# The attention output product of the second layer as one level of Strassen

## The chip, the cores and the metric

The kernel runs on one core of one Trainium2 chip. It is one launch that computes two layers. The metric is device time in microseconds, the median of the runs of one kernel.

## The reference

512 tokens of width 1024, all float32. The first layer is a differential attention beside a bidirectional retention, an output product and a residual. The second layer is the one that the change touches, cut to what matters here:

```python
h = rms_norm(x, norm_g)
u = h @ w_in
v_c, b_c, c_c, z_c, q, k, v, z_a, gate_logits = split(u)
y_c = b_c * causal_depthwise_conv(c_c * v_c, conv_w) * silu(z_c)
y_a = y_c @ w_conv_out
o = sliding_window_attention(rms(q), rms(k), v, sinks) * silu(z_a)   # 512 x 1024
y_b = o @ w_attn_out                                                 # 1024 x 1024 weights
gates = sigmoid(gate_logits + gate_b)
g_a, g_b = split(gates)
return x + (g_a * y_a + g_b * y_b) @ w_out
```

## The kernel before, in words

**Products.** Every large product is taken from float32r parts: a number is split into hi (rounded) and lo (the rest), and `products` issues three matmuls, hi x hi, hi x lo and lo x hi. TensorE works through the weights in pieces of 512 KB, numbered `n`; a piece is 24 matmuls. Four pieces make a unit `u`. Units 0 to 13 are the projections of both layers and the output product of the first. Units 14 to 21 (`U_CONV`, pieces 56 to 87) are the convolution branch, 22 and 23 (`U_AOUT`, pieces 88 to 95) the attention output product, 24 and 25 (`U_COUT`, 96 to 103) the convolution output product. In these pieces one matmul has 512 columns, the tokens, and a piece gives 128 of the 1024 output columns. From piece 104 (`GATES`) on, the gate product and the last output product are already done as one level of Strassen, with 7 products of half size where 8 blocks would be needed: a gate piece has matmuls of 256 columns (tokens), again 24. Sums of weight blocks for these lie in a DRAM scratch, `w_sums`, four blocks of 512 x 512 for each group (groups 0 and 1 the gates, 2 the last product).

**The way of a weight piece.** SP loads it into one of 4 ring slots (more from the gate stage on) as soon as `piece_done` says that the piece 4 before it is done, GpSimd rounds it to hi (`round_piece`, L723), VectorE subtracts for lo (`split_piece`, L1142), and TensorE waits for `w_split`. From piece 110 on ScalarE rounds (`round_block`, L835). Rounding and split of piece n+3 stand in the program at piece n.

**The order of the other work.** It is written by hand: every piece has two halves, and `STEPS` lists for each half the steps (transposes, scores, attention products) that TensorE does after it and that the other engines serve in the same order. The second layer's sliding window attention has 16 steps k = 0 to 15, one for each three halves from piece 53 (`WIN_FIRST`) on. In phase 0 TensorE does the scores S2 of step k and then AV2, the product with the values, of step k-2; in phase 1 TP, the transposes of the probabilities of step k-1. After TP, ScalarE and VectorE take the transposes as hi and lo, and GpSimd masks them (`part_keys`, L734 and L738: one select each for hi and lo where there is one key tile, two each otherwise); AV2 waits for that by `pT_split`. The steps OS at pieces 80 to 83 split the gated attended values `gT2` into `o2_hi` and `o2_lo`.

**The sums of weight blocks.** SP copies blocks of w_in_2 and w_out_2 into `w_sums` (`copy_block`, L666, 1 MB each) at pieces 20 to 27 and 48 to 51 (`COPY_AT`). GpSimd then adds blocks to them by DMAs that accumulate (`gather`, L751, 1 MB each), four steps for each group, one at the end of every third piece from 56 to 89 (`SUM_AT`). From step 2 of a group on, `gather` waits until the earlier steps of the group have landed:

```python
if step >= 2:
    pool.wait_ge(w_gathered[group], 16 * step)
source = (w_block(group, 0, 1), w_sums[4 * group], w_block(group, 0, 1), w_sums[4 * group + 1])[t]
pool.dma_start(w_sums[4 * group + t], source, accum_op=ALU.add).then_inc(w_gathered[group], 16)
```

**Banks.** Tiles of a plain unit go to the four banks of `proj`; ScalarE evacuates those of U_AOUT to `y_b` and of U_COUT to `part` with a factor of 0.5 (L968). The gate products use all eight banks in turn (`gate_banks`).

Of the kernel before, what the change touches and what calls it, by code (L numbers as in the profile page):

```python
# [30 lines left out]
P = 128  # L31
# [26 lines left out]
U_AOUT = U_CONV + KC  # L58
U_COUT = U_AOUT + KC // 4
UNITS = U_COUT + KC // 4  # L60
GATES = 4 * UNITS
# [7 lines left out]
GROUPS = 3  # L69
# [27 lines left out]
def slot_of(n):  # L97

    if n < GATES:
        return n % SLOTS  # L100
    return RING + n - GATES if n < GATES + EARLY else (n - GATES - EARLY) % RING
# [15 lines left out]
def unit_columns(u):  # L117
# [10 lines left out]
    if u < U_AOUT:  # L128
        t = u - U_CONV
        return TRA, [("w_in_2", c + P * t) for c in (CV, CC, CB, CZ)]  # L130
    t = 4 * ((u - U_AOUT) % (KC // 4))
    return TRA, [("w_attn_out_2" if u < U_COUT else "w_conv_out_2", P * (t + j)) for j in range(4)]

# [12 lines left out]
X_AGAIN_AT = range(4 * U_O0 + 3, 4 * U_O0 + 7)  # L146
XS_HOOKS = (7, 7, 8, 9)
# [117 lines left out]
def tiles_done(n, half):  # L265

    u, q = divmod(n, 4)
    if n >= GATES:
        return []
# [5 lines left out]
def build(nc, a):  # L275
    with ExitStack() as ctx:
# [121 lines left out]
        m_hi = sb("m_hi", [P, KC, S], F32R, stack=later)  # L398
        logit = sb("logit", [P, 2, 2, 2, 256], stack=later)
# [35 lines left out]
        v_sum = spare[:, 0:2, 256:512]  # L435

# [10 lines left out]

        def pair_of(t, c, r):

            return t[:].rearrange("p (h k) s -> p k h s", h=2)[:, c, :, r * 256:r * 256 + 256]  # L450

        def w_block(group, row, col):

            w, c = (("w_in_2", G2), ("w_in_2", G2 + D), ("w_out_2", 0))[group]
# [14 lines left out]
        def ring_parts(n, i):  # L469

            t = ring(n)[i]
            if n >= FINAL:
# [3 lines left out]
        def sources(n):  # L476

            if n >= FINAL:
# [5 lines left out]
        def wait_room(eng, n):  # L484
# [7 lines left out]
            elif n >= GATES:  # L492
                eng.wait_ge(piece_done, 4 * U_COUT)
# [41 lines left out]
        hi_done = sem("hi_done"); block_hi_done = sem("block_hi_done")  # L535
# [42 lines left out]
        w_copied = sem("w_copied"); w_gathered = [sem(f"w_gathered{i}") for i in range(GROUPS)]  # L578
        minus_done = sem("minus_done"); low_landed = [sem(f"low_landed{i}") for i in range(len(LOW_BY_DMA))]
        sx_summed = sem("sx_summed"); sx_hi_done = sem("sx_hi_done"); sx_split = sem("sx_split")  # L580
# [8 lines left out]
        def wait_tile(eng, u, j):  # L589
# [3 lines left out]
            else:  # L593
                eng.wait_ge(piece_done, 4 * u + j + 1)
# [20 lines left out]

        N_PARAMS = 18
# [4 lines left out]
        def _(sp):  # L621
            def load_piece(n):
                u, q = divmod(n, 4)
                raw, landed = ring(n)[0], raw_landed[slot_of(n)]
                if n >= GATES:
# [37 lines left out]
            def copy_block(i):  # L663

                t, group = divmod(i, GROUPS)
# [1418 lines left out]
```

## Time and profile before

| what | us |
|---|---|
| median of 3 runs (816.49 to 817.74) | 817.2 |
| the profiled execution, its own time | 816.7 |
| its span, first to last instruction | 814.7 |
| TensorE busy | 808.5 |
| VectorE busy | 609.4 |
| ScalarE busy | 321.9 |
| GpSimd busy | 182.6 |

The profile is of one execution. Its times count from the start of the span. Matmuls are pipelined and their ends are modelled, so the duration of one matmul in the profile is longer than the distance from one to the next; the distance is what a matmul costs. Instructions that issue a DMA count as no busy time.

### The profile page before, as it was taken

The numbers are of one execution on the slowest core, as the hardware profiler recorded it, in microseconds if no ns is written. First come the engines' busy times: TensorE is split into PE (matmuls) and PEld (weight loads), VectorE is DVE, ScalarE is ACT, GpSimd is POOL, SyncE is SP. The second block draws the span as 40 slices with busy tenths as digits, with TensorE's granted clock in tenths as the row PEclk, the third lists the DMA queues.
The fourth block names the chain that finished last, engine by engine and source line by source line (L and its number), as shares of the span: only waits on it lengthen the run. The fifth ranks groups of instructions, "written<-read, shape, count | busy, mean of one in ns | idle before, by whom it ended". The sixth has DMA issues, their size and how long they took to land.

```text
span 814.7 us, 11429 instructions
## 1 busy us (share of the span) xinstructions
PE 808.5 (99%) x4220; PEld 687.1 (84%) x4220; DVE 609.4 (75%) x1096; ACT 321.9 (40%) x701; POOL 182.6 (22%) x189
## 2 busy tenths in 40 slices
PE   9999999999999999999999999999999999999998
PEld 7778888888888888888888888888888888999986
DVE  4998778768984476885579788978952269599998
ACT  4374465632212255334445554441000122355580
POOL 2212111111111221121324445444323224000000
PEclk9999999999999999999999999999999999999999
DMA  7332214445143222653365555566876335866562
GB/s 239 87 97 77 79 52 153 158 157 179 53 155 126 82 83 77 208 175 90 91 130 130 125 119 120 128 130 155 168 165 158 104 88 145 233 182 183 182 205 78
DMA packets 129565, 108.92 MB, mean 134 GB/s; under 512 B 4525, under 2 KB 101350, under 8 KB 129510
## 3 DMA queue, kind: packets, MB, share of 16 engines
q1 hardware_dynamic: 123142, 95.60, 38.4%
q0 software_dynamic: 6336, 12.58, 9.4%
q8 instruction: 34, 0.56, 0.3%
q14 instruction: 21, 0.17, 0.1%
q10 hardware_dynamic: 32, 0.01, 0.0%
HBM read 106.08 MB, written 27.26 MB: 164 GB/s over the span
## 4 chain that ended last, share of the span: by engine, by line
PE 92%; DVE 5%; issue 1%; ACT 1%; DVEq 0%; ACTq 0%
PE proj L1736 24%; PE proj L1738 24%; PE proj L1737 24%; PE bank_t L1750 3%; PE bank_o L1825 2%; DVE x L1447 1%; DVE w_lo L1142 1%; PE score L1738 1%; PE score L1737 1%; PE score L1736 1%; PE score L1900 1%; PE score L1899 1%; PE score L1811 1%; PE score L1810 1%; PE bank_o L1918 1%
## 5 line engine op out<-in xcount | busy, mean ns | idle before, releaser
L723 POOL TENSOR_SCALAR w_hi<-w_raw 128x1024 fp32r<-128x1024 f32 x109 | 128.8, 1182 | 436.2 <-DMA w_raw<-in_w_in_dram 310.8
L1142 DVE TENSOR_TENSOR w_lo<-w_raw,w_hi 128x1024 fp32r<-128x1024 f32 x145 | 179.9, 1244 | 60.2 <-POOL w_hi L723 59.6
L1736 PE MATMUL proj<-xt_hi,w_hi 128*128 128x512 f32 (+1 forms) x448 | 171.1, 382 | 0.0
L1738 PE MATMUL proj<-xt_hi,w_lo 128*128 128x512 f32 (+1 forms) x448 | 168.1, 375 | 0.0
L1737 PE MATMUL proj<-xt_lo,w_hi 128*128 128x512 f32 (+1 forms) x448 | 167.8, 375 | 0.0
L1738 PEld LDWEIGHTS proj<-xt_hi,w_lo 128*128 128x128 f32 x448 | 84.4, 188 | 15.5
L1737 PEld LDWEIGHTS proj<-xt_lo,w_hi 128*128 128x128 f32 x448 | 84.5, 189 | 14.2
L1736 PEld LDWEIGHTS proj<-xt_hi,w_hi 128*128 128x128 f32 x448 | 84.5, 189 | 13.9
L1736 PE MATMUL proj<-w_hi,xt_hi 128*128 128x512 f32 x152 | 61.0, 401 | 0.2 <-ACT prob L922 0.2
L1738 PE MATMUL proj<-w_hi,xt_lo 128*128 128x512 f32 x152 | 59.5, 392 | 0.0
L1737 PE MATMUL proj<-w_lo,xt_hi 128*128 128x512 f32 x152 | 59.4, 391 | 0.0
L835 ACT ACTIVATE w_hi<-w_raw 128x1024 fp32r<-128x1024 f32 x36 | 36.9, 1049 | 9.6 <-DMA w_raw<-w_sums 3.8
L1736 PE MATMUL proj<-w_hi,yc_hi 128*128 128x512 f32 x96 | 38.9, 406 | 0.0
L1738 PE MATMUL proj<-w_hi,yc_lo 128*128 128x512 f32 x96 | 37.6, 392 | 0.0
L1737 PE MATMUL proj<-w_lo,yc_hi 128*128 128x512 f32 x96 | 37.4, 390 | 0.0
L1736 PEld LDWEIGHTS proj<-w_hi,xt_hi 128*128 128x128 f32 x152 | 28.6, 188 | 6.9 <-ACT prob L922 0.7
L1038 ACT ACTIVATE prob<-prob,neg_mx 128x512 f32<-128x512 f32 x32 | 22.9, 716 | 28.3 <-DVE neg_mx L1546 28.3
L1080 ACT ACTIVATE prob<-prob,neg_m 128x128 f32<-128x128 f32 x64 | 25.0, 391 | 22.3 <-DVE sink_m L1652 22.3
L1738 PEld LDWEIGHTS proj<-w_hi,xt_lo 128*128 128x128 f32 x152 | 28.5, 188 | 6.2
L1737 PEld LDWEIGHTS proj<-w_lo,xt_hi 128*128 128x128 f32 x152 | 28.6, 188 | 6.0 <-issue 0.2
L734 POOL TENSOR_SCALAR_AFFINE_SELECT yc_hi<-pT 128x512 fp32r<-128x512 f32 x28 | 17.6, 646 | 71.4 <-ACT pT L1094 71.4
L1543 DVE CUSTOM_DVE_ANT_0 prob<-score,table 128x512 f32<-128x512 f32 x32 | 20.8, 688 | 16.1 <-PE score L1811 16.1
(420 smaller groups left out, 1774.4 us busy)
## 6 DMA issues: line engine op xcount, KB each, us to landing
w_raw<-in_w_in_dram SPq DMA_DIRECT2D x79, 512.0 KB, 3.8
w_sums<-in_w_in_dram SPq DMA_DIRECT2D x8, 1024.0 KB, 7.5
w_raw<-w_sums SPq DMA_DIRECT2D x32, 256.0 KB, 3.3
w_raw<-in_w_out_dram SPq DMA_DIRECT2D x14, 512.0 KB, 3.3
w_raw<-in_w_in_dram SPq DMA_DIRECT2D x26, 256.0 KB, 3.6
w_sums<-w_sums POOLq DMA_DIRECT2D x6, 1024.0 KB, 9.9
w_sums<-in_w_out_dram SPq DMA_DIRECT2D x4, 1024.0 KB, 6.8
w_sums<-in_w_in_dram POOLq DMA_DIRECT2D x4, 1024.0 KB, 9.9
```

Source lines behind the costliest of these rows:

```text
L723: pool.tensor_scalar(hi, raw, 1.0, 1.0, ALU.mult, ALU.mult).then_inc(hi_done, 1)
L734: pool.affine_select(out=pT_hi[:, c, :, :], in_=pT[:, 0, :, :], compare_op=op, fill=0.0, base=base, pattern=pattern, channel_multiplier=step)
L835: act.activation(hi, raw, ACT.Copy).then_inc(block_hi_done, 1)
L1038: act.activation(prob[:, m % 2, mp, :], prob[:, m % 2, mp, :], ACT.Exp, bias=neg_mx[:, m % 2, mp:mp + 1], accum_out=den[:, m % 2, mp:mp + ...
L1080: act.activation(prob2[:, m % 2, r, 0:P], prob2[:, m % 2, r, 0:P], ACT.Exp, bias=neg_m2[:, m % 4, r:r + 1], accum_out=den2[:, m % 4, r:r + 1])
L1142: dve.tensor_tensor(lo, raw, hi.bitcast(F32), ALU.subtract).then_inc(w_split, 1)
L1543: dve.tensor_tensor_reduce(prob[:, sl, mp, :], score[:, mp, :], table[:, h % 2, CENTRE - i * P:CENTRE - i * P + S], 1.0, -3e38, ALU.subtra ...
L1736: pe.matmul(out, left[0], right[0], start=first, stop=False)
L1737: pe.matmul(out, left[0], right[1], start=False, stop=False)
L1738: return pe.matmul(out, left[1], right[0], start=False, stop=last)
L1750: last = pe.transpose(dst, src, ident[:])
L1825: last = pe.matmul(bank_o[:, i * P:(i + 1) * P], wT[:, m % 2, c * P:(c + 1) * P], va[:, c, h * P:(h + 1) * P], start=(c == 0), stop=(c == 3))
```

## The change

The attention output product becomes one level of Strassen. It has 14 pieces instead of 8, 88 to 101: two pairs, each with the 7 products in the order of `OUT_ORDER`. Each piece gives 2 x 128 output columns for 256 tokens over 512 of the 1024 rows, 24 matmuls of 256 columns (`attended_product`). The convolution output is then pieces 102 to 109, and the gates begin at 110. The unit U_AOUT is gone.

- Weights: a fourth group (`ATTENDED`) of block sums of w_attn_out_2. All 16 copies stand at pieces 12 to 27. All 16 gathers stand at pieces 53, 54, 56, 57, 59, 60 and so on to 75, the new group first. SP waits for that group's gathers before it loads piece 88.
- The 14 pieces are rounded by ScalarE (`round_out`), the rest as before.
- Attended values: ScalarE takes the hi copies of OS from VectorE, for 256 tokens only in chunks 0 to 3. VectorE forms four sums of quarters in place (`attended_sum`, pieces 85 to 87), ScalarE rounds them (pieces 87 and 88), VectorE takes their low parts (`attended_low`, pieces 88 to 90). The factor 0.5 of the evacuation moves into the gating (0.25).
- Results: VectorE adds up the products from PSUM into `y_b` (`combine_out`), ScalarE copies the first of each pair (`take_first_out`).
- Waits for banks and for the end of this stage move accordingly.

```diff
-U_AOUT = U_CONV + KC
-U_COUT = U_AOUT + KC // 4
+U_COUT = U_CONV + KC
 UNITS = U_COUT + KC // 4
-GATES = 4 * UNITS
+AOUT = 4 * U_COUT
+OUT_PIECES = 7 * 2
+COUT = AOUT + OUT_PIECES
+GATES = 4 * UNITS + OUT_PIECES
...
+OUT_ORDER = [A11, A12, A22, S2, S1, S4, S3]
+GROUPS = 4
+ATTENDED = 3
...
-COPY_AT = [*range(4 * U_GA, 4 * U_O0), *range(4 * U_Z0, 4 * U_Z1)]
-SUM_AT = [4 * U_Z1 + 4 + 3 * i for i in range(4 * GROUPS)]
+COPY_AT = range(4 * U_RQK, 4 * U_O0)
+GROUP_ORDER = [ATTENDED, 0, 1, 2]
+SUM_AT = [4 * U_Z1 + 1 + 3 * i // 2 for i in range(4 * GROUPS)]
...
+SO_SUM_AT = ((AOUT - 3, 1), (AOUT - 2, 0), (AOUT - 2, 1), (AOUT - 1, 0))
+SO_HI_AT = ((AOUT - 1, 0), (AOUT - 1, 1), (AOUT, 0), (AOUT, 1))
+SO_LOW_AT = ((AOUT, 0), (AOUT, 1), (AOUT + 1, 1), (AOUT + 2, 1))
...
+        def sum_of_attended(product):
+            place = {S2: 0, S1: 1, S4: 2}
+            if product == S3:
+                return [quarter(t, 1, 0) for t in (o2_hi, o2_lo)]
+            return [t[:, 4 * place[product]:4 * place[product] + 4, :] for t in (so_hi, so_lo)]
+        def left_of_attended(product):
+            source, chunk, token = LEFT[product]
+            if source:
+                return sum_of_attended(product)
+            return [t[:, chunk:chunk + 4, token:token + 256] for t in (o2_hi, o2_lo)]
...
+                pair, i = divmod(n - AOUT, 7)
+                return [right_of(ATTENDED, OUT_ORDER[i])[:, 256 * pair:256 * pair + 256].rearrange("(k p) c -> p k c", p=P)]
...
+        def out_bank(x):
+            return gate_banks[(x + SLOTS) % 8]
...
-                t, group = divmod(i, GROUPS)
-                sp.dma_start(w_sums[4 * group + t], w_block(group, *((0, 0), (1, 1), (1, 1), (1, 0))[t])).then_inc(w_copied, 16)
+                group, t = GROUP_ORDER[i // 4], i % 4
+                sp.dma_start(w_sums[4 * group + t], w_block(group, *((0, 0), (1, 1), (1, 1), (1, 0))[t])).then_inc(w_copied[group], 16)
...
+                if n == AOUT:
+                    sp.wait_ge(w_gathered[ATTENDED], 16 * 4)
...
-                group, step = divmod(i, 4)
+                group, step = GROUP_ORDER[i // 4], i % 4
                 t = (0, 2, 1, 3)[step]
-                if i == 0:
-                    pool.wait_ge(w_copied, 16 * 4 * GROUPS)
+                if step == 0:
+                    pool.wait_ge(w_copied[group], 16 * 4)
                 if step >= 2:
                     pool.wait_ge(w_gathered[group], 16 * step)
...
-                            round_piece(m)
+                            if not AOUT <= m < COUT:
+                                round_piece(m)
...
+            def round_out(n):
+                raw, hi, _ = ring(n)
+                act.wait_ge(raw_landed[slot_of(n)], 16 * landings(n))
+                wait_room(act, n)
+                act.activation(hi, raw, ACT.Copy).then_inc(out_hi_done, 1)
...
+            def take_first_out(pair):
+                act.wait_ge(yc_done, KC)
+                if pair:
+                    act.wait_ge(out_combined, COMBINED[S2])
+                act.wait_ge(piece_done, AOUT + 7 * pair + 1)
+                act.activation(u_sum, out_bank(7 * pair), ACT.Copy).then_inc(out_first, 1)
...
+                    if (n, half) in SO_HI_AT:
+                        product, after_sums = ((S2, 3), (S1, 1), (S4, 4), (S3, 2))[SO_HI_AT.index((n, half))]
+                        act.wait_ge(so_summed, after_sums)
+                        act.activation(sum_of_attended(product)[0], raw_sum(product), ACT.Copy).then_inc(so_hi_done, 1)
+                    if half == 1 and AOUT <= n + SPLIT_AHEAD < COUT:
+                        round_out(n + SPLIT_AHEAD)
+                    if half == 1 and AOUT <= n < COUT:
+                        if (n - AOUT) % 7 == 0:
+                            take_first_out((n - AOUT) // 7)
...
+                        elif kind == "OS":
+                            act.wait_ge(o2_gated, WIN_STEPS)
+                            tokens = slice(0, 256 if m < 4 else S)
+                            act.activation(o2_hi[:, m, tokens], gT2[:, m, tokens], ACT.Copy).then_inc(o2_hi_done, 1)
...
+            def attended_sum(i):
+                x11, x12, x21, x22 = (quarter(gT2, row, col) for row in range(2) for col in range(2))
+                if i == 0:
+                    dve.wait_ge(o2_split, KC)
+                    dve.tensor_tensor(x22, x22, x21, ALU.subtract).then_inc(so_summed, 1)
+                elif i == 1:
+                    dve.wait_ge(so_summed, 1)
+                    dve.tensor_tensor(x21, x11, x21, ALU.subtract).then_inc(so_summed, 1)
+                elif i == 2:
+                    dve.wait_ge(so_summed, 2)
+                    dve.scalar_tensor_tensor(out=x11, in0=x22, scalar=-1.0, in1=x11, op0=ALU.mult, op1=ALU.subtract).then_inc(so_summed, 1)
+                else:
+                    dve.wait_ge(so_summed, 3)
+                    dve.scalar_tensor_tensor(out=x12, in0=x12, scalar=-1.0, in1=x11, op0=ALU.mult, op1=ALU.subtract).then_inc(so_summed, 1)
...
+            def attended_low(i):
+                product = (S2, S1, S4, S3)[i]
+                dve.wait_ge(so_hi_done, i + 1)
+                hi, lo = sum_of_attended(product)
+                dve.tensor_tensor(lo, raw_sum(product), hi.bitcast(F32), ALU.subtract).then_inc(so_split, 1)
...
+            def combine_out(x):
+                pair, i = divmod(x, 7)
+                product = OUT_ORDER[i]
+                if product in (A11, A22):
+                    return
+                psum, kept = out_bank(x), out_bank(7 * pair + OUT_ORDER.index(A22))
+                def out(r, h):
+                    return y_b[:, 4 * h + 2 * pair:4 * h + 2 * pair + 2, 256 * r:256 * r + 256]
+                dve.wait_ge(piece_done, AOUT + x + 1)
+                if product == A12:
+                    dve.wait_ge(out_first, pair + 1)
+                else:
+                    dve.wait_ge(out_combined, 7 * pair + COMBINED[product] - (2 if product == S3 else 1))
+                if product == A12:
+                    dve.tensor_tensor(out(0, 0), u_sum, psum, ALU.add).then_inc(out_combined, 1)
+                elif product == S2:
+                    dve.tensor_tensor(w_sum, u_sum, psum, ALU.add).then_inc(out_combined, 1)
+                elif product == S1:
+                    dve.wait_ge(so_split, 4)
+                    dve.tensor_tensor(v_sum_out, w_sum, psum, ALU.add).then_inc(out_combined, 1)
+                elif product == S4:
+                    dve.scalar_tensor_tensor(out=out(0, 1), in0=v_sum_out, scalar=-1.0, in1=psum, op0=ALU.mult, op1=ALU.subtract).then_inc(out_combined, 1)
+                elif product == S3:
+                    dve.scalar_tensor_tensor(out=out(1, 1), in0=v_sum_out, scalar=-1.0, in1=psum, op0=ALU.mult, op1=ALU.subtract).then_inc(out_combined, 1)
+                    dve.tensor_tensor(w_sum, w_sum, psum, ALU.add).then_inc(out_combined, 1)
+                    dve.wait_ge(out_combined, 7 * pair + 6)
+                    dve.tensor_tensor(out(1, 0), w_sum, kept, ALU.add).then_inc(out_combined, 1)
...
-                        done(dve.tensor_copy(o2_hi[:, m, :], gT2[:, m, :]))
-                        dve.tensor_tensor(o2_lo[:, m, :], gT2[:, m, :], o2_hi[:, m, :].bitcast(F32), ALU.subtract).then_inc(o2_split, 1)
+                        dve.wait_ge(o2_hi_done, m + 1)
+                        tokens = slice(0, 256 if m < 4 else S)
+                        dve.tensor_tensor(o2_lo[:, m, tokens], gT2[:, m, tokens], o2_hi[:, m, tokens].bitcast(F32), ALU.subtract).then_inc(o2_split, 1)
...
+            def attended_product(x):
+                n = AOUT + x
+                product = OUT_ORDER[x % 7]
+                wait_low(n)
+                if x == 0:
+                    pe.wait_ge(o2_split, KC)
+                if x < 4:
+                    wait_evacuated(pe, U_COUT - 1, x)
+                elif x < 6:
+                    pe.wait_ge(score2_read, WIN_STEPS)
+                elif x == 6:
+                    pe.wait_ge(pT_split, WIN_STEPS)
+                elif x == 7:
+                    pe.wait_ge(o2_summed, 2 * WIN_STEPS)
+                else:
+                    wait_combined_out(x - 8)
+                if x < 7 and LEFT[product][0]:
+                    pe.wait_ge(so_split, (S2, S1, S4, S3).index(product) + 1)
+                left = left_of_attended(product)
+                w = [ring_parts(n, i)[0] for i in (1, 2)]
+                for j in range(2):
+                    for k in range(4):
+                        last = products(out_bank(x)[:, j, :], [t[:, k, j * P:(j + 1) * P] for t in w], [t[:, k, :] for t in left], k == 0, k == 3)
+                last.then_inc(piece_done, 1)
...
-                if x < 2:
-                    pe.wait_ge(score2_read, WIN_STEPS)
-                elif x == 2:
-                    pe.wait_ge(pT_split, WIN_STEPS)
-                elif x == 3:
-                    pe.wait_ge(o2_summed, 2 * WIN_STEPS)
-                elif x < 8:
+                if x == 0:
+                    pe.wait_ge(out_combined, OUT_PIECES)
+                if 4 <= x < 8:
```

## Rows read from the trace of the kernel before

**Rows 1.** The page's busy times: engine, us, share of the span, instructions

```profile
PE 808.5 (99%) x4220; PEld 687.1 (84%) x4220; DVE 609.4 (75%) x1096; ACT 321.9 (40%) x701; POOL 182.6 (22%) x189
```

**Rows 2.** The table by stage: busy us and instructions per engine, clock, DMA

```profile
403.80:548.90 145.10, 145.10 (x716) 121.89 (x715) 119.54 (x222) 72.89 (x241) 66.10 (x78) 1.00 0.58 127
548.90:604.60 55.70, 55.70 (x249) 46.15 (x248) 43.26 (x54) 3.75 (x7) 20.86 (x18) 1.00 0.71 156
```

**Rows 3.** TensorE in order of time (start us, us), two stage starts

```profile
604.61 0.39 PE L1736 MATMUL proj<-o_hi,w_hi 128*128 128x512 f32 x1
...
648.13 0.39 PE L1736 MATMUL proj<-yc_hi,w_hi 128*128 128x512 f32 x1
```

**Rows 4.** TensorE in order of time, gate products 0 and 9

```profile
691.65 0.28 PE L1736 MATMUL score<-xt_hi,w_hi 128*128 128x256 f32 x1
...
717.56 0.28 PE L1736 MATMUL score<-sx_hi,w_hi 128*128 128x256 f32 x1
```

**Rows 5.** The chain that ended last, share of the span by engine

```profile
PE 92%; DVE 5%; issue 1%; ACT 1%; DVEq 0%; ACTq 0%
```

**Rows 6.** The DMA issues: queue, count, KB each, median us to landing

```profile
w_raw<-w_sums SPq DMA_DIRECT2D x8, 512.0 KB, 3.5
```

**Rows 7.** The page's costliest groups: busy us, mean ns, idle before

```profile
L1142 DVE TENSOR_TENSOR w_lo<-w_raw,w_hi 128x1024 fp32r<-128x1024 f32 x145 | 179.9, 1244 | 60.2 <-POOL w_hi L723 59.6
...
L835 ACT ACTIVATE w_hi<-w_raw 128x1024 fp32r<-128x1024 f32 x36 | 36.9, 1049 | 9.6 <-DMA w_raw<-w_sums 3.8
```

**Rows 8.** Groups of VectorE by line, 652 to 733 us

```profile
L1348 DVE TENSOR_TENSOR sx_lo<-sx,sx_hi 128x1024 fp32r<-128x1024 f32 x4 | 5.6, 1398 | 0.1
...
L1367 DVE TENSOR_TENSOR acc<-th,bank_t 128x512 f32<-128x512 f32 x1 | 0.7, 689 | 1.1 <-PE bank_t L1738 1.1
```

**Rows 9.** SP's copies into w_sums, time from issue to landing

```profile
DMA to landing us min/median/max: 6.1/7.3/8.6
```

**Rows 10.** GpSimd in order of time around piece 63

```profile
449.46 1.06 POOL L751 DMA_DIRECT2D w_sums<-w_sums  x1
450.18 1.43 POOL L723 TENSOR_SCALAR w_hi<-w_raw 128x1024 fp32r<-128x1024 f32 x1
456.68 1.22 POOL L734 TENSOR_SCALAR_AFFINE_SELECT yc_hi<-pT 128x512 fp32r<-128x512 f32 x2 [5.07 <-ACT pT L1094]
457.86 1.22 POOL L738 TENSOR_SCALAR_AFFINE_SELECT yc_lo<-pT 128x512 fp32r<-128x512 f32 x2
```

**Rows 11.** GpSimd's gathers, all twelve, and then those of 445 to 540 us

```profile
L751 POOL DMA_DIRECT2D w_sums<-in_w_in_dram x4: 1056/1067/1209, 406.6 to 513.1; - x4
...
DMA to landing us min/median/max: 9.0/9.9/12.1
...
DMA to landing us min/median/max: 9.4/9.8/10.1
```

**Rows 12.** GpSimd in order of time around pieces 69 and 75

```profile
490.42 2.20 POOL L738 TENSOR_SCALAR_AFFINE_SELECT yc_lo<-pT 128x512 fp32r<-128x512 f32 x2
492.57 1.06 POOL L751 DMA_DIRECT2D w_sums<-in_w_in_dram  x1
...
533.95 1.05 POOL L751 DMA_DIRECT2D w_sums<-w_sums  x1
```

**Rows 13.** TensorE in order of time: second attention products, AV2

```profile
420.68 0.40 PE L1918 MATMUL bank_o<-yc_hi,v 128*128 128x512 f32 x1
...
461.89 0.40 PE L1918 MATMUL bank_o<-yc_hi,v 128*128 128x512 f32 x1
...
504.01 0.40 PE L1918 MATMUL bank_o<-yc_hi,v 128*128 128x512 f32 x1
...
545.18 0.39 PE L1918 MATMUL bank_o<-yc_hi,v 128*128 128x512 f32 x1
```

**Rows 14.** SP's load at 450.6 us, and its load at 437.4 us, to landing

```profile
DMA to landing us min/median/max: 9.7/9.7/9.7
...
DMA to landing us min/median/max: 3.8/3.8/3.8
```

More of the change, by code:

```diff
@@ L127, in unit_columns @@
             (TRA, [("w_in_2", Z2 + 512 + P * j) for j in range(4)])][u]
-    if u < U_AOUT:
+    if u < U_COUT:
         t = u - U_CONV
         return TRA, [("w_in_2", c + P * t) for c in (CV, CC, CB, CZ)]
-    t = 4 * ((u - U_AOUT) % (KC // 4))
-    return TRA, [("w_attn_out_2" if u < U_COUT else "w_conv_out_2", P * (t + j)) for j in range(4)]
+    return TRA, [("w_conv_out_2", P * (4 * (u - U_COUT) + j)) for j in range(4)]
 UNIT = [unit_columns(u) for u in range(UNITS)]
@@ L577, in build @@
         act_chain = sem("act_chain"); dve_chain = sem("dve_chain"); pool_chain = sem("pool_chain")
-        w_copied = sem("w_copied"); w_gathered = [sem(f"w_gathered{i}") for i in range(GROUPS)]
+        w_copied = [sem(f"w_copied{i}") for i in range(GROUPS)]; w_gathered = [sem(f"w_gathered{i}") for i in range(GROUPS)]
         minus_done = sem("minus_done"); low_landed = [sem(f"low_landed{i}") for i in range(len(LOW_BY_DMA))]
+        o2_hi_done = sem("o2_hi_done")
+        so_summed = sem("so_summed"); so_hi_done = sem("so_hi_done"); so_split = sem("so_split")
+        out_first = sem("out_first"); out_combined = sem("out_combined")
         sx_summed = sem("sx_summed"); sx_hi_done = sem("sx_hi_done"); sx_split = sem("sx_split")
@@ L840, in take_first @@
             def take_first(c):
-                act.wait_ge(yc_done, KC)
+                act.wait_ge(out_combined, OUT_PIECES)
                 if c:
@@ L983, in _ @@
                         gate_step(n - GATES)
[L984 to L985 removed]
+                    if (n, half) in SO_HI_AT:
[7 more added lines that the diff above has]
+                            take_first_out((n - AOUT) // 7)
+                    if half == 1 and COUT + 2 <= n < COUT + 6:
+                        q = n - COUT - 2
                         act.wait_ge(sx_summed, (4, 6, 8, 10)[q])
@@ L1691, in _ @@
                         left_lows(c)
-                    if half == 1 and 0 <= n - 4 * U_COUT < 5:
-                        input_sums(n - 4 * U_COUT)
-                    if half == 1 and 0 <= n - 4 * U_COUT - 3 < 4:
-                        input_low(n - 4 * U_COUT - 3)
+                    if half == 1 and AOUT <= n < COUT:
+                        combine_out(n - AOUT)
+                    if half == 1 and 0 <= n - COUT < 5:
+                        input_sums(n - COUT)
+                    if half == 1 and 0 <= n - COUT - 3 < 4:
+                        input_low(n - COUT - 3)
                     if n >= FINAL and (n - FINAL) % 2:
@@ L1717, in _ @@
                         take_tiles(n, half)
-                    if half == 1 and WIN_FIRST <= n < 4 * U_AOUT and not splits_wait(n, half):
+                    if half == 1 and WIN_FIRST <= n < AOUT and not splits_wait(n, half):
                         for m in ROUNDED_AT[n]:
                             split_piece(m)
+                    if (n, half) in SO_LOW_AT:
+                        attended_low(SO_LOW_AT.index((n, half)))
+                    if (n, half) in SO_SUM_AT:
+                        attended_sum(SO_SUM_AT.index((n, half)))
                     if (n, half) == (0, 0):
@@ L1933, in _, with wait_combined_out @@
             keep_busy(1)
+            def wait_combined_out(x):
+                pair, i = divmod(x, 7)
+                if i == 0:
+                    pe.wait_ge(out_first, pair + 1)
+                else:
+                    pe.wait_ge(out_combined, 7 * pair + COMBINED[OUT_ORDER[i]])
+            def attended_product(x):
[12 more added lines that the diff above has]
+                    pe.wait_ge(o2_summed, 2 * WIN_STEPS)
+                else:
+                    wait_combined_out(x - 8)
[7 more added lines that the diff above has]
+                last.then_inc(piece_done, 1)
             for n in range(GATES):
-                u, q = divmod(n, 4)
+                if AOUT <= n < COUT:
+                    attended_product(n - AOUT)
+                    continue
+                u, q = unit_piece(n)
                 slot = n % SLOTS
```

77 lines of the change are left out of this document (45 added, 32 removed).

## The prediction

> **What bounds the kernel now.** I read the shares of busy time first. TensorE is busy for 99% of the span [rows 1], but that figure is modelled, so the second view was the table by stage: TensorE's row is full in both stretches from 403.80 to 604.60, at a granted clock of 1.00, the full level, 2.4 GHz [rows 2]. The third view, TensorE's own order of time, shows what one product costs. The attention output product begins at 604.61 and the convolution output product at 648.13 [rows 3]: 43.52 us for 8 pieces x 24 = 192 matmuls of 512 columns, 0.2267 us each, with no gap at either end. In the gate stage, which is already one level of Strassen, product 0 begins at 691.65 and product 9 at 717.56 [rows 4]: 25.91 us for 9 x 24 = 216 matmuls of 256 columns, 0.1200 us each. The chain of waits is 92% TensorE [rows 5]; its DVE part lies mostly after 769 us, behind everything this change touches. So a removed matmul is worth its full period, and a stall of TensorE anywhere between 60 and 770 us costs its full length. The other engines matter where TensorE waits for them in order.
>
> **The product itself.** Removed: 192 matmuls, 43.52 us. Added: 14 pieces x 2 x 4 x 3 = 336 matmuls of 256 columns, 336 x 0.1200 = 40.3 us. Gain: 3.2 us. That is only 7%, where 7/8 of the columns would give 12.5% (5.4 us), because 512 columns cost 0.2267 us and 256 cost 0.1200, more than half.
>
> The Trainium skill, page TensorE: Matmul & The Clock Gate, section Back-to-back issue gap, gives 518 cycles for 512 columns and 262 for 256; at 2.4 GHz an estimate from it is 41.4 us less 36.7, a gain of 4.8 us. The trace's periods are both some 11 ns longer than that page's, and I use the trace's.
>
> **Does the new stage hold its pace?** A piece now lasts 24 x 0.12 = 2.88 us instead of 5.44, with the same 4 slots. A load is issued when the piece 4 before it ends, so load, rounding and low part must fit in 3 x 2.88 = 8.64 us. Loads from w_sums land in 3.5 us [rows 6], ScalarE's rounding takes 1.05, VectorE's low part 1.24 [rows 7]: 5.8 us, so 2.8 us are left for queueing. VectorE has 14 low parts (17.4 us), 4 low parts of the sums of attended values (4 x 1.40 = 5.6, by the row of sx_lo) and 14 PSUM additions of 0.69 (9.7) [rows 7, 8]: 32.7 us in 40.3. Followed in program order, the closest approach is at pieces 90 and 91: ScalarE first does the last tanh, two roundings of sums and then the piece, VectorE the last convolution tile. I get 1.0 to 1.5 us of margin. PSUM banks are reused 8 products later, over 2 us after their last reader. I take 0 here. The bound above: if each of 14 pieces came 0.5 us late, 7 us. The bound below is 0, since nothing on TensorE's path gets shorter here but the matmuls. The four sums (4 x 1.24, at most 1.40) and ScalarE's 8 hi copies lie 12 us and more ahead of the product, where VectorE is busy 43.26 of 55.70 us and ScalarE 3.75 [rows 2]. That VectorE loses the 8 copies of the attended values is worth nothing, it does not hold TensorE there.
>
> **The copies (SP's queue).** 16 copies of 1 MB at pieces 12 to 27 instead of 12 at 20 to 27 and 48 to 51. Each is queued behind a load and lands in 6.1 to 8.6 us [rows 9]. The next load is issued 5.4 to 10 us behind a copy, so it meets at most the copy's last 3 us and lands that much later than its usual 3.8 us, of some 16 us of lead. Cost 0; bound above 1 us. SP also waits once more, at piece 88, for the gathers of the attention block; queued behind it is every later load, but those gathers are over some 180 us earlier: 0. The new waits for out_combined (ScalarE before the convolution output's tiles, TensorE before gate product 0) lie one and eight pieces behind the last addition: 0.
>
> **The gathers (GpSimd's queue).** Here is what I think decides. Before, a gather is issued at the end of every third piece; after, at the end of pieces 53, 54, 56, 57, 59, 60 and so on to 75. Of each group of four, step 3 reads what step 2 wrote, so GpSimd waits for step 2 to land before it issues step 3. Before, 21 us lay between the two, and the wait cost nothing. After, step 2 is issued at the end of pieces 56, 62, 68, 74 and step 3 one piece later, where GpSimd arrives after only the rounding of one piece (450.18 to 451.6 [rows 10]). The gathers land 9.4 to 10.1 us after issue in this stretch [rows 11]. Queued behind the waiting GpSimd are the masks of the next probabilities (part_keys), whose pT_split TensorE waits for in the second attention product, AV2. Those instructions, four selects, last 2.44 us [rows 10], and the issue holds GpSimd 0.72 us (449.46 to 450.18).
>
> So AV2 can start at (issue of step 2) + landing + 0.72 + 2.44. The issue points exist in the trace of before, since pieces 62, 68, 74 had a gather too: 449.46, 492.57, 533.95 [rows 10, 12]. The AV2 that follows starts at 461.89, 504.01, 545.18 [rows 13]. With a landing of 9.8, 9.8 and 10.1:
> - piece 63: 462.42 against 461.89, stall 0.5 us
> - piece 69: 505.53 against 504.01, stall 1.5 us
> - piece 75: 547.21 against 545.18, stall 2.0 us
> - piece 57: the first block row has one key tile and no previous one, two selects, half of the 2.44; issue 406.6, landing 9.9, ready 418.4, needed 420.68 [rows 11, 13]: no stall.
>
> Sum 4.1 us. That is the lower value. The selects are slower when VectorE is busy: the second pair takes 2.20 us at 490.42 instead of 1.22 [rows 10, 12], 1.0 us more for each of three, 7.1 us. Step 1 now follows step 0 by some 2 us, and a load issued while a gather runs lands only with it (9.7 us against 3.8 [rows 14]); the rounding ahead of the next masks, and with it step 2, can come up to 1 to 1.5 us late, 11 us in all at worst. Bound below: 0, if the gather were over by the time that GpSimd would be free anyway. The issue itself keeps GpSimd for 0.72 us at four more places, where nothing is due: 0. I take 5.6 us, the middle of 4.1 and 7.1, since the masks run contended about half of the time.
>
> **Sum.** -3.2 + 5.6 + 0 + 0 = +2.4 us. The profiled execution took 816.7 us (span 814.7), the median is 817.2, so the sum goes on the median: 819.6 us.
>
> **The rivals.** A difference under 0.2% (1.6 us, 815.6 to 818.8) is not to be told from none.
> - *The gather's wait decides, as above* (chance 0.50): 818.9 to 824, likeliest 819.6. It holds as long as step 2 takes over 9.6 us: the three issue-to-need gaps less 3.16 us are 9.3, 8.3 and 8.1 us, so stalls add up to 3 x landing - 25.6, which equals 3.2 at 9.6 us.
> - *The two cancel* (0.20): a landing near 9.6 us, or masks that run quickly: 817.2, 815.6 to 818.8.
> - *The wait is hidden, the kernel is faster* (0.22). Mechanism: the gather lands in 8.1 us or less and GpSimd is back before the masks are due. Then all of the 3.2 us stays: 814.0. For it: before, no gather had anything waiting on it, and GpSimd is busy only 66 of 145 us in that stretch [rows 2]. Against: no gather of the twelve landed in under 9.0 us [rows 11].
> - *The new stage cannot hold 2.88 us per piece* (0.08): 7 us on top of the likeliest, or 824 to 826. For: TensorE never had pieces this short with ScalarE in front of VectorE and 4 slots. Against: 5.8 of 8.64 us.
>
> By the Trainium skill, page DMA: Bandwidth & Descriptors, section Anatomy of one DMA, a transfer issued by GpSimd takes 2.0 us plus bytes / 436e3; an estimate for 1 MB is 4.4 us, and by that the wait would be hidden and 814.0 would come out. The trace does not agree: its gathers, which accumulate from memory to memory, land in 9.0 to 12.1 us.
>
> **Chances and range.** Faster 0.23: the hidden wait, and a little of partial hiding. Same 0.25: cancelling, and the lower edge of the first case. Slower 0.52: the rest. Since cases of both signs hold most of the chance, the range runs from the hidden wait to the first case with contended masks and late loads, 813.8 to 824.0; the likeliest case alone has 818.0 to 823.0.
>
> **What would show it.** Right: in the profile after, the output product takes 40.3 us for 336 matmuls; TensorE has idle time or a longer period at AV2 at three places, with the masks as releaser, starting 10 us after a gather; GpSimd shows the masks right behind the issue of step 3. Wrong: the gather's landing is short of 9 us, the attention steps keep their period of 10.5 us, or VectorE's low parts are late in the output product, then seen as TensorE waiting for w_lo there.

## The result, and the profile after

| | us | ratio to before, 95% interval |
|---|---|---|
| before, median of 6 (816.49 to 817.74) | 816.99 | |
| after, median of 6 (829.04 to 835.57) | 832.48 | 1.0187 [1.0159, 1.0215] |
| after, span of the profiled execution | 833.8 | before: 814.7 |

The change makes the kernel 15.5 us slower; 2.4 us more were forecast, 819.6 us, in a range of 813.8 to 824.0. The profiled execution of after is the slowest of the six (835.57, with a mean granted clock of 0.990 where the others have 0.991 to 0.995), so its rows add up to 19.1 us, not 15.5.

The page of the kernel after: the chain by engine, which answers to [rows 5].

```profile
PE 75%; issue 9%; DVE 7%; POOL 5%; ACT 2%; DMA 1%; DVEq 0%; POOLq 0%; ACTq 0%
```

TensorE's part has fallen from 92% to 75%, and GpSimd, which was not in the chain, is in it with 5%. The list of waits of the kernel after says for what:

```profile
POOL w_sums L803 <- DMA w_sums<-w_sums: 35.8, 4, 9.9
...
PE bank_o L2063 <- POOL yc_lo L790: 14.0, 4, 4.6
```

GpSimd waits four times, 35.8 us in all, for gathers to land, and TensorE waits four times, 14.0 us in all, for masks. Neither row exists before. The places, by TensorE's order of time after:

```profile
422.97 0.50 PE L2063 MATMUL bank_o<-yc_hi,v 128*128 128x512 f32 x1 [2.11 <-POOL yc_lo L790]
...
468.92 0.80 PE L2063 MATMUL bank_o<-yc_hi,v 128*128 128x512 f32 x1 [4.47 <-POOL yc_lo L790]
...
516.57 0.50 PE L2063 MATMUL bank_o<-yc_hi,v 128*128 128x512 f32 x1 [2.79 <-POOL yc_lo L790]
...
564.55 0.79 PE L2063 MATMUL bank_o<-yc_hi,v 128*128 128x512 f32 x1 [4.63 <-POOL yc_lo L790]
```

These are the second attention products (AV2) 2, 6, 10 and 14, the first ones behind the gathers at pieces 57, 63, 69 and 75; they answer to the four of [rows 13]. The table by stage over this part of the kernel after (length in us, TensorE busy with its instructions, granted clock, DMA share, GB/s):

```profile
420.00:424.00 4.00, 1.89 (x12) 1.00 0.59 107
424.00:457.00 33.00, 33.00 (x164) 1.00 0.83 173
457.00:475.00 18.00, 13.53 (x58) 0.81 0.76 140
475.00:507.00 32.00, 31.87 (x159) 1.00 0.73 157
507.00:522.00 15.00, 12.21 (x53) 0.89 0.83 157
522.00:554.00 32.00, 31.97 (x159) 1.00 0.75 156
554.00:571.00 17.00, 12.37 (x49) 0.80 0.74 141
```

The granted clock is 1.00 between the waits, and 0.81, 0.89 and 0.80 in the stretches that hold the waits of 4.47, 2.79 and 4.63 us. Right behind the second wait TensorE's matmuls of 512 columns stand 0.43 us apart:

```profile
470.79 0.63 PE L1881 MATMUL proj<-xt_hi,w_hi 128*128 128x512 f32 x1
471.22 0.63 PE L1882 MATMUL proj<-xt_lo,w_hi 128*128 128x512 f32 x1
471.65 0.63 PE L1883 MATMUL proj<-xt_hi,w_lo 128*128 128x512 f32 x1
```

At the full level it is 0.2267 us [rows 3]; 0.43 us is the lower level, 1.2 GHz. So each of these three waits costs twice, once while it lasts and once more behind it. The first wait, 2.11 us, does not: the clock stays at 1.00 there.

Where the 19.1 us come from, by the distance between the first and the last transposes TP of the window attention: 393.72 to 570.38 us after, 393.7 to 548.8 before, 176.7 against 155.1, so +21.6 us. In it: 14.0 us of waits; by the three long periods between neighbouring TPs (17.36, 15.19 and 16.55 us, where the same periods of before are 10.53, 10.53 and 9.54) less their waits, 2.36 + 1.87 + 2.38 = 6.6 us for the clock; the last 1.0 us are small ones. The output product gives back: it runs from 626.16 to 666.47 after, 40.3 us against 43.5, -3.2 us. The remaining 0.7 us lie behind it, of them 0.5 us one wait at piece 103.

GpSimd around piece 63 after, which answers to [rows 10]:

```profile
446.72 1.04 POOL L775 TENSOR_SCALAR w_hi<-w_raw 128x1024 fp32r<-128x1024 f32 x1 [5.87 <-DMA w_raw<-in_w_in_dram]
448.19 1.89 POOL L775 TENSOR_SCALAR w_hi<-w_raw 128x1024 fp32r<-128x1024 f32 x1 [0.43 <-DMA w_raw<-in_w_in_dram]
450.03 2.21 POOL L786 TENSOR_SCALAR_AFFINE_SELECT yc_hi<-pT 128x512 fp32r<-128x512 f32 x2
452.20 1.22 POOL L790 TENSOR_SCALAR_AFFINE_SELECT yc_lo<-pT 128x512 fp32r<-128x512 f32 x2
453.37 1.05 POOL L803 DMA_DIRECT2D w_sums<-w_sums  x1
454.07 1.42 POOL L775 TENSOR_SCALAR w_hi<-w_raw 128x1024 fp32r<-128x1024 f32 x1
465.42 1.04 POOL L803 DMA_DIRECT2D w_sums<-w_sums  x1 [9.92 <-DMA w_sums<-w_sums]
466.10 1.61 POOL L786 TENSOR_SCALAR_AFFINE_SELECT yc_hi<-pT 128x512 fp32r<-128x512 f32 x2
467.27 1.59 POOL L790 TENSOR_SCALAR_AFFINE_SELECT yc_lo<-pT 128x512 fp32r<-128x512 f32 x2
```

This is the predicted order, step by step: gather, one rounding, a wait of 9.92 us, the next gather 0.68 us, the masks, and then TensorE goes on at 468.92. But two roundings in front of the first masks are late here. The first of them waits for the load of 432.4 us, which landed only after 14.3 us, while two gathers (issued at 429.5 and 431.7) were in flight. The loads of weight pieces between 400 and 560 us after, time from issue to landing:

```profile
DMA to landing us min/median/max: 3.6/4.7/15.3
```

### The profile page after: what moved, and what is told of

Its sections match the earlier page's. It is cut to its first block, busy times and chain, and to the rows that moved or that the text cites. A ratio compares the mean times of both kernels' runs of the same rounds, so it can differ in the third digit from the quotient of the medians.

```text
span 833.8 us, 11790 instructions
## 1 busy us (share of the span) xinstructions
PE 813.2 (98%) x4364; PEld 696.0 (83%) x4364; DVE 632.5 (76%) x1116; ACT 340.0 (41%) x721; POOL 178.7 (21%) x185
## 4 chain that ended last, share of the span: by engine, by line
PE 75%; issue 9%; DVE 7%; POOL 5%; ACT 2%; DMA 1%; DVEq 0%; POOLq 0%; ACTq 0%
PE proj L1881 19%; PE proj L1883 19%; PE proj L1882 19%; PE bank_t L1895 2%; DVE w_lo L1225 2%; POOL w_hi L775 2%; PE bank_o L1970 1%; POOL yc_lo L790 1%; POOL yc_hi L786 1%; DVE x L1585 1%; PE score L1883 1%; PE score L1882 1%; PE score L1881 1%; DMA w_raw<-in_w_in_dram 1%; PE score L1956 1%
## 5 line engine op out<-in xcount | busy, mean ns | idle before, releaser
L1225 DVE TENSOR_TENSOR w_lo<-w_raw,w_hi 128x1024 fp32r<-128x1024 f32 x151 | 190.3, 1264 | 40.9 <-POOL w_hi L775 32.6
L775 POOL TENSOR_SCALAR w_hi<-w_raw 128x1024 fp32r<-128x1024 f32 x101 | 119.4, 1199 | 461.1 <-DMA w_raw<-in_w_in_dram 326.9
L1882 PE MATMUL proj<-xt_lo,w_hi 128*128 128x512 f32 (+1 forms) x448 | 169.5, 378 | 0.0
L1882 PEld LDWEIGHTS proj<-xt_lo,w_hi 128*128 128x128 f32 x448 | 85.4, 191 | 14.6
L1681 DVE CUSTOM_DVE_ANT_0 prob<-score,table 128x512 f32<-128x512 f32 x32 | 20.8, 689 | 15.3 <-PE score L1956 15.3
L1163 ACT ACTIVATE prob<-prob,rec 128x128 f32<-128x128 f32 x64 | 20.5, 391 | 24.6 <-DVE rec L1794 24.6
```

The source lines that it names most:

```text
L775: pool.tensor_scalar(hi, raw, 1.0, 1.0, ALU.mult, ALU.mult).then_inc(hi_done, 1)
L1163: last = act.activation(prob2[:, m % 2, r, 0:P], prob2[:, m % 2, r, 0:P], ACT.Copy, scale=rec2[:, m % 4, r:r + 1])
L1225: dve.tensor_tensor(lo, raw, hi.bitcast(F32), ALU.subtract).then_inc(w_split, 1)
L1681: dve.tensor_tensor_reduce(prob[:, sl, mp, :], score[:, mp, :], table[:, h % 2, CENTRE - i * P:CENTRE - i * P + S], 1.0, -3e38, ALU.subtra ...
L1882: pe.matmul(out, left[0], right[1], start=False, stop=False)
```

## The experiments

Eleven variants ran, on three chips. Each ratio is to the kernel before on the same chip, where it took 817.3 to 817.5 us. The kernel after was measured beside a before of 816.99, so between kernels the ratios compare better than the times.

**E1. The groups take turns, so that step 3 stands three pieces behind step 2.** On the kernel after:

```diff
-                group, step = GROUP_ORDER[i // 4], i % 4
+                group, step = GROUP_ORDER[2 * (i // 8) + i % 2], i % 8 // 2
```

> The changed kernel with its gathers at the same 16 places and of the same size, but the groups of a pair take turns, so that step 3 of a group stands three pieces behind its step 2 instead of one. Theory A (GpSimd's wait for the gather's landing in front of the masks costs the window stage its 21.6 us): no wait of GpSimd for w_sums, the 16 attention steps take 155 to 159 us instead of 176.7, time 813.5 to 817. Rival B (the density of the gathers, 8 MB more in the memory's way, with loads that land in 10 to 15 us, costs it): no gain or under 5 us, time 827 to 832. Rival C (the new product stage is the loss): unchanged at 832.

Measured: 822.05 us, 1.0057 [1.0034, 1.0080]. GpSimd's wait for w_sums is gone, and 10.4 of the 18 us between the kernel after and the best version below are back. 7 to 8 us are not: in time, neither A nor B as stated. In the profile the window attention takes 158.7 us, inside A's 155 to 159. Masks are still late at three places (0.80, 1.39 and 1.57 us), now because the rounding in front of them waits for loads that land late (8 to 16 us). The profile is of an execution of 819.86 us at a clock of 1.00; what the median has on top of it, 2.2 us, no trace shows.

**E2. The same gathers, spread evenly over pieces 53 to 85.** On the kernel after:

```diff
-SUM_AT = [4 * U_Z1 + 1 + 3 * i // 2 for i in range(4 * GROUPS)]
+SUM_AT = [4 * U_Z1 + 1 + 35 * i // 16 for i in range(4 * GROUPS)]
```

> The changed kernel with its 16 gathers in the old order of groups but spread evenly over pieces 53 to 85, two or three pieces between neighbours instead of 1.5. Theory A: step 3 stands two pieces (over 11 us) behind step 2 and the gather has landed, no wait of GpSimd, 813.5 to 815. Rival B: density falls by a third, so also faster, and faster than the kernel whose groups take turns by some us. Rival C: unchanged at 832.

Measured: 814.94 us, 0.9972 [0.9962, 0.9982], faster than before. The window attention takes 155.1 us between the first and the last TP, as before. Rival C, a loss by the new product stage, falls. A and B both allow this time, so this run does not separate wait from density. "No wait of GpSimd" was missed: it waits 8.16 us once, for the last gather but one to land before it issues the last at 598.41, where no masks are due. One stall of 1.2 us is left at piece 90, in the place where the prediction had the smallest margin; the last gather, issued at 598.41, was still in flight when that piece was loaded (issued at 599.38, landed after 10.0 us).

**E3. Only the dense gathers, without the new product.** On the kernel before, whose 12 gathers go to the first 12 places of the kernel after:

```diff
-SUM_AT = [4 * U_Z1 + 4 + 3 * i for i in range(4 * GROUPS)]
+SUM_AT = [4 * U_Z1 + 1 + 3 * i // 2 for i in range(4 * GROUPS)]
```

> The kernel before, without the Strassen product, with its 12 gathers at the places of the changed kernel's first 12 (53, 54, 56, 57, 59, 60 and so on to 69). Theory A: step 3 waits at pieces 57, 63 and 69, three stalls of TensorE; by the changed kernel's first three (2.4, 6.8 and 4.9 us with what the clock loses) 831 us. Rival C: 817.

Measured: 828.56 us, 1.0136 [1.0110, 1.0161]. The loss needs nothing of Strassen. GpSimd waits 24.6 us in three places; TensorE waits 1.36, 2.34, 0.44 and 2.39 us. 831 had been expected from the kernel after; the single waits are shorter here. The clock stays at 1.00 behind the wait of 2.34 us and falls behind that of 2.39 (0.89 between 505 and 520 us), whose period is 1.8 us longer than the wait explains.

**E4. Only the early copies.** On the kernel before:

```diff
-COPY_AT = [*range(4 * U_GA, 4 * U_O0), *range(4 * U_Z0, 4 * U_Z1)]
+COPY_AT = range(4 * U_RQK, 4 * U_RQK + 12)
```

> The kernel before with its 12 copies into w_sums at pieces 12 to 23 instead of 20 to 27 and 48 to 51, nothing else. All theories: same as before, 816.5 to 818; a rival that puts a part of the loss on the copies beside the first attention expects over 818.5.

Measured: 817.48 us, 1.0001 [0.9992, 1.0011]. These 12 early copies cost nothing; all 16 stand early in E2, E5 and E11, which come out as forecast for the product alone or within 1 us of it.

**E5. A gather at the end of every second piece.** On the kernel after:

```diff
-SUM_AT = [4 * U_Z1 + 1 + 3 * i // 2 for i in range(4 * GROUPS)]
+SUM_AT = range(4 * U_Z1 + 1, 4 * U_Z1 + 1 + 8 * GROUPS, 2)
```

> The changed kernel with its 16 gathers at the end of every second piece, 53, 55, 57 and so on to 83. Theory A: attention steps at 155.1 us as in the evenly spread kernel, and the last gather has landed before piece 90 is loaded, so the stall of 1.2 us there goes too; left are the product's 3.2 us of gain less 0.5 us at piece 103: 0.996 to 0.997 of the kernel before, 813.9 to 814.9. Rival: the stall at piece 90 is the new stage's own, then it stays, as before 0.9972.

Measured: 814.43 us, 0.9961 [0.9948, 0.9975]. TensorE's order of time shows the output product stage from its first matmul to the first of the convolution output:

```profile
605.10 0.28 PE L1881 MATMUL proj<-o_hi,w_hi 128*128 128x256 f32 x1
...
645.41 0.40 PE L1881 MATMUL proj<-yc_hi,w_hi 128*128 128x512 f32 x1
```

40.31 us for 336 matmuls, 0.1200 each, as forecast, and no wait at piece 90: the stall of E2 came with the gather, not from the stage alone. GpSimd waits once here for a gather, behind the last attention step:

```profile
577.45 1.04 POOL L803 DMA_DIRECT2D w_sums<-w_sums  x1 [5.08 <-DMA w_sums<-in_w_out_dram]
```

TensorE has no wait there. So 5 us of GpSimd's waiting cost nothing where nothing is due from it.

**E6. Only the wait, at the old density.** On the kernel before: 12 gathers as before, but step 3 of each group one piece behind step 2.

```diff
-SUM_AT = [4 * U_Z1 + 4 + 3 * i for i in range(4 * GROUPS)]
+SUM_AT = [56, 59, 62, 63, 68, 71, 74, 75, 80, 83, 86, 87]
```

> The kernel before, its 12 gathers at 56, 59, 62, 63, 68, 71, 74, 75, 80, 83, 86, 87: the density is the same, only step 3 of each group is put one piece behind step 2. The prediction's formula (issue + 9.8 us of landing + 0.72 + 2.44 for the masks) gives stalls of 0.5 to 1.5 us at piece 63 and 2.0 to 3.0 at 75, none in the convolution part: with up to 2 us more where the clock falls, 819.5 to 823. If a wait at low density costs as much as in the changed kernel (6.8 us for one), 829. Rival (density alone): 817.5.

Measured: 822.3 us, 1.0058 [1.0045, 1.0072]. This is the prediction's formula by itself. TensorE's waits in this kernel:

```profile
463.87 0.50 PE L1918 MATMUL bank_o<-yc_hi,v 128*128 128x512 f32 x1 [0.81 <-POOL yc_lo L738]
...
549.67 0.50 PE L1918 MATMUL bank_o<-yc_hi,v 128*128 128x512 f32 x1 [2.25 <-POOL yc_lo L738]
```

0.81 and 2.25 us, where the formula had 0.5 to 1.5 and 2.0 to 3.0. The table by stage of the same kernel shows what comes on top:

```profile
460.00:470.00 10.00, 9.20 (x47) 1.00 0.92 190
...
550.00:560.00 10.00, 10.00 (x40) 0.83 0.64 133
```

Behind the wait of 0.81 us the clock stays; behind that of 2.25 us it is 0.83, and the period there is 13.71 us instead of 9.55: 2.25 us of wait and 1.9 us of clock.

**E7. Only the pairs: two gathers in flight, nothing to wait for.** On the kernel before:

```diff
-SUM_AT = [4 * U_Z1 + 4 + 3 * i for i in range(4 * GROUPS)]
+SUM_AT = [59, 60, 65, 68, 71, 72, 77, 80, 83, 84, 89, 92]
```

> The kernel before, its 12 gathers at 59, 60, 65, 68, 71, 72, 77, 80, 83, 84, 89, 92: steps 0 and 1 of a group stand one piece apart as in the changed kernel, steps 2 and 3 stand three pieces apart, so GpSimd never waits for a gather. Theory A (only the wait costs): 817.5. Theory D (two gathers in flight make a weight load land after 14 us, and with it the rounding in front of the masks comes late): masks late by 1 to 2 us at pieces 62 and 74, TensorE stalls by up to 1.5 us each, 817.5 to 820.5, and the load at piece 61 lands in 12 to 15 us.

Measured: 817.9 us, 1.0007 [0.9998, 1.0016], no change. The load at piece 61 landed after 14.3 us, as theory D had it, but no mask was late enough to stop TensorE: the stalls of D did not come. By the interval the three pairs together cost at most 1.3 us when GpSimd never waits for a gather.

**E8. GpSimd rounds the 14 pieces.** On E5:

```diff
-                            if not AOUT <= m < COUT:
-                                round_piece(m)
+                            round_piece(m)
...
-                if AOUT <= n < COUT:
-                    dve.wait_ge(out_hi_done, n - AOUT + 1)
-                elif n < ROUNDED_BY_ACT:
-                    dve.wait_ge(hi_done, n + 1 - (OUT_PIECES if n >= COUT else 0))
+                if n < ROUNDED_BY_ACT:
+                    dve.wait_ge(hi_done, n + 1)
...
-                    if half == 1 and AOUT <= n + SPLIT_AHEAD < COUT:
-                        round_out(n + SPLIT_AHEAD)
```

> The changed kernel with gathers at every second piece, and the 14 pieces of the attention output product rounded by GpSimd instead of ScalarE. Rounding takes 1.05 to 1.2 us on either; GpSimd has nothing else there, ScalarE has the last tanh and four roundings of sums. Theory A: the same time within 0.1%, or up to 1 us faster if ScalarE's queue is what brings piece 90 late. Rival (ScalarE's rounding is needed to hold 2.88 us per piece): slower by 1 us or more.

Measured: 817.27 us, 0.9996 [0.9987, 1.0005]: the gain is gone, the rival was right. By the profile the stage takes 42.04 us (606.78 to 648.82) instead of 40.31. TensorE waits there 0.52 and 0.22 us for low parts. Another 0.9 us lies in the window attention (one wait of 0.55 us for masks) and 0.8 us ahead of it, where the edit changes nothing; why is not settled.

**E9. TensorE is kept at work while it waits.** On the kernel after; the added matmuls compute nothing that is used.

```diff
+                    if m in (6, 10, 14):
+                        pe.wait_ge(o2_summed, 2 * m)
+                        for _ in range(20 if m == 10 else 34):
+                            pe.matmul(bank_o[:, 0:256], xt_hi[:, 0, 0:P], xt_hi[:, 0, 0:256], start=True, stop=True)
                     pe.wait_ge(pT_split, m + 1)
```

> The changed kernel with work that nobody needs on TensorE while it waits: 34, 20 and 34 matmuls of 256 columns (0.12 us each, so 4.1, 2.4 and 4.1 us) into bank_o just ahead of the second attention products 6, 10 and 14, where the trace shows waits of 4.5, 2.8 and 4.6 us. The third part of the loss is by my theory the clock that falls after these waits (attention step periods of 17.4, 15.2 and 16.6 us, of which 10.5, 10.5 and 9.7 are work and 4.5, 2.8 and 4.6 waiting: 2.3, 1.9 and 2.3 us). Then the granted clock stays at 1.00 and 5 to 6.5 us come back: 826 to 828. Rival: those 6 us are contention on other engines, then the time stays at 832 or grows.

Measured: 829.93 us, 1.0160 [1.0142, 1.0178]. 826 to 828 was missed, and since this interval overlaps that of the kernel after, the 2.6 us between the medians are not clear of noise. What the run shows, it shows in its profile. The first wait was not filled:

```profile
423.01 0.50 PE L2067 MATMUL bank_o<-yc_hi,v 128*128 128x512 f32 x1 [1.88 <-POOL yc_lo L790]
```

The table by stage, first behind this wait, then at the filled places:

```profile
423.00:430.00 7.00, 6.99 (x26) 0.76 0.88 164
...
460.00:470.00 10.00, 10.00 (x66) 1.00 0.95 184
510.00:520.00 10.00, 10.00 (x61) 1.00 0.81 160
560.00:570.00 10.00, 10.00 (x53) 1.00 0.69 145
```

The clock stays at 1.00 around the three filled places, and their periods are 14.61, 12.93 and 13.66 us instead of 17.36, 15.19 and 16.55: what before takes there plus the time of the added matmuls, no more. So the rival, contention on other engines, falls for these places. Behind the unfilled wait of 1.88 us the clock is 0.76 and the period 13.8 us, so 1.9 us of clock were lost there, where none were in the profile of after. The window attention takes 171.0 us instead of 176.7; that compares executions of 829.95 and 835.57 us.

**E10. Half gathers.** On the kernel after; the sums of weight blocks are formed for half of their columns only.

```diff
-                pool.dma_start(w_sums[4 * group + t], source, accum_op=ALU.add).then_inc(w_gathered[group], 16)
+                pool.dma_start(w_sums[4 * group + t][:, 0:256], source[:, 0:256], accum_op=ALU.add).then_inc(w_gathered[group], 16)
```

> The changed kernel, its gathers at their places but each of half the columns (256 of 512, 0.5 MB), so the sums of weight blocks are only half formed. If the landing is in proportion to bytes past some 2 to 3 us, it takes 6 to 6.5 us and GpSimd is back before the masks are due: 814 to 816. If it is mostly fixed, 9 us or more, the waits stay: 825 or more.

Measured: 817.92 us (814.86 to 821.39), 1.0005 [0.9991, 1.0019]. The gathers' time to landing, here and in the kernel after:

```profile
DMA to landing us min/median/max: 5.6/6.7/9.4
```

```profile
DMA to landing us min/median/max: 8.2/9.9/14.5
```

The median is 3.2 us less for half the bytes; a straight line through both, an estimate, gives some 3.5 us fixed (6.7 less 3.2) and the rest for bytes. GpSimd's waits fall from 35.8 to 18.8 us, and of the 18.0 us between the kernel after and E11 below 14.6 are back. The profile is of an execution of 814.86 us; TensorE waits 0.28 and 0.35 us for masks in it. 814 to 816 was expected, and where the 3 us more of the median lie, no trace shows.

**E11. All gathers one piece later.** On the kernel after, one character:

```diff
-SUM_AT = [4 * U_Z1 + 1 + 3 * i // 2 for i in range(4 * GROUPS)]
+SUM_AT = [4 * U_Z1 + 2 + 3 * i // 2 for i in range(4 * GROUPS)]
```

> The changed kernel with all 16 gathers one piece later (54, 55, 57, 58 and so on to 76): the same density, the same waits of GpSimd for the landing, but step 3 now stands right behind the masks of a step instead of right ahead of them. Theory A with placement: GpSimd still waits 30 to 40 us for gathers, but TensorE's long waits go, what is left is the loss by density alone as in the kernel whose groups take turns: 818 to 824. Rival (a wait hurts wherever it stands): 830 or more.

Measured: 814.47 us, 0.9966 [0.9954, 0.9977], as good as E5, at the full density; 818 to 824 had been expected. GpSimd around a group's steps 2 and 3:

```profile
453.94 1.06 POOL L803 DMA_DIRECT2D w_sums<-w_sums  x1
457.84 1.22 POOL L786 TENSOR_SCALAR_AFFINE_SELECT yc_hi<-pT 128x512 fp32r<-128x512 f32 x2 [2.84 <-ACT pT L1175]
459.01 1.22 POOL L790 TENSOR_SCALAR_AFFINE_SELECT yc_lo<-pT 128x512 fp32r<-128x512 f32 x2
460.21 1.48 POOL L775 TENSOR_SCALAR w_hi<-w_raw 128x1024 fp32r<-128x1024 f32 x1
463.07 1.06 POOL L803 DMA_DIRECT2D w_sums<-w_sums  x1 [1.37 <-DMA w_sums<-w_sums]
```

The masks and a rounding now lie between step 2 and step 3, and only 1.37 us are left to wait. The waits for gathers sum to 8.0 us, not to the 30 to 40 that I had expected; so this kernel does not show that a long wait in a harmless place is free; the single ones of 5.08 us in E5 and 8.16 us in E2 are all there is for that. It shows that density is not the cause: rival B falls, and with it the reading of E1's remainder as density. In E11 no weight load takes over 7.7 us, in E1 up to 16.3 us, with the same number of gathers in the same time. Gathers here are issued about 7 us or more apart, there in pairs 2 us apart.

## Why the prediction was wrong

**The product** (336 x 0.1200 us, gain 3.2 us): right, 40.3 us in the kernel after and 40.31 in E5. With the gathers out of the way the whole change gives 0.9961, 3.2 us.

**The pace of the new stage** (cost 0, margin 1.0 to 1.5 us at pieces 90 and 91): right for the kernel after, and the place was right: E2's stall there, 1.2 us, came only with a gather beside it. The margin does depend on ScalarE's rounding (E8).

**The copies** (0): right, shown for 12 of the 16 (E4).

**The gathers** (5.6 us, with 4.1 as the lower value and 11 at worst): this is the step that failed. The direction and the mechanism were right: the mechanism is the one described, and the formula holds when nothing else changes (E6: 0.81 and 2.25 us). It holds in the kernel after too, once that kernel's own issues and landings go in: 422.3, 468.3, 515.9 and 563.8 us for the four AV2, which start at 422.97, 468.92, 516.57 and 564.55. The term was mis-sized: it measured 21.6 us in the profile, and 18.7 by the medians (15.5 and the product's 3.2). Four things were short:

- *The issue of step 2.* I took it from the trace before. After TP it comes 5.8, 6.5, 7.1 and 7.0 us, before it came 2.9, 5.0, 6.0 and 5.2 us after its TP (403.76, 444.5, 486.6 and 528.73). A load behind two gathers is late (14.3 us), its rounding is late with it, and the roundings stand in front of the masks and the gather in GpSimd's queue. I had allowed 1 to 1.5 us for this and left it out of the value.
- *Piece 57.* "No stall" rested on 406.6 us for the issue. It became 409.55, and there were 2.11 us of wait.
- *The landing.* 9.8 to 10.1 us were assumed; at steps 2 of the kernel after it was 10.8, 11.8, 9.9 and 10.7 us.
- *The clock.* The sum had no term for it. 6.6 of the 21.6 us in the profile come from the lower level behind three of the waits. E9's profile bears this out place by place; its median does not size it. The other executions of after have a higher mean clock, so this part is likely smaller in them; no trace sizes it there.

The landing that I called decisive (9.6 us for break-even) is therefore not the right border: even E10's 6.7 us only brings the kernel to the time of before.

Between the kernel after and E11 lie one piece of shift and 18.0 us, so the place of the gathers costs all of it. How it splits is less sure. E1 removes the wait for step 2 and gives back 10.4 us; it is still 7.6 us over E11. Its profile has 5.3 us of that, nearly all in the window attention and at the late mask right behind its last TP. But E1 has seven pairs of gathers 2 us apart where the kernel after has three, so its late roundings are not those of the kernel after.

By the Trainium skill, page DMA: Bandwidth & Descriptors, section Anatomy of one DMA, an estimate is 4.4 us for 1 MB and 3.2 us for 0.5 MB. The runs have medians of 9.9 and 6.7 us for accumulating transfers between places in memory, so here the measurement decides.

## What to carry to other kernels

An in-order queue that issues DMAs and also does short work for the bottleneck engine needs a schedule by distance: before moving a DMA whose issue waits for another DMA, count what stands between the two and what stands right behind the second. Here the same change loses 15.5 us or gains 3 us, by one piece of shift in its sixteen transfers. Size such a wait by a trace with the new traffic in it, not by issue times and landings of the old one, and allow for what TensorE's clock can cost behind a wait: up to 2.4 us behind a wait of 1.9 to 4.6 us here, though not behind every one.

## What was not expected of the hardware

- After waits of 1.88 us (E9), 2.25 us (E6), 2.39 us (E3) and 2.79 to 4.63 us (the kernel after) TensorE's granted clock fell, in the kernel after with matmuls of 512 columns 0.43 us apart instead of 0.227; 1.8 to 2.4 us were lost each time. After waits of 0.81 us (E6), 2.11 us (the kernel after) and 2.34 us (E3) it did not fall. So the length of the wait alone does not tell the two apart.
- A weight load of 0.5 MB issued within some 1 us of the second of two accumulating gathers, themselves 2 us apart, lands after 14.3 to 15.3 us in the kernel after, and after 14.3 and 11.1 us in E7. Issued behind a single one, it lands after 8.1 to 10.8 us in the kernel before (seven times of eight), and after some 3.7 us with no gather beside it.
- An accumulating transfer of 1 MB inside the memory takes 9.9 us (median), one of 0.5 MB 6.7 us.
